# A GELU spelled out over three engines instead of one ScalarE activation, in a hybrid attention and state-space block

## The reference, cut to what matters

```python
y = s5_scan(u, ...)                    # includes the term d * u
z = jax.nn.gelu(y)                     # the tanh form
o_s5 = z * jax.nn.sigmoid(z @ w_glu[l] + b_glu[l])
branch_b = (o_s5 * jax.nn.silu(gate_s5)) @ w_proj_s5[l]
```

## Time and profile before

| | before |
|---|---|
| median of 3 runs | 458.5 us (458.2 to 458.8) |
| the profiled execution | 459.13 us, its span 457.3 us |
| TensorE busy | 422.7 us, 92% of the span |
| VectorE busy | 286.0 us, 63% |
| ScalarE busy | 201.8 us, 44% |
| GpSimd busy | 154.0 us, 34% |
| clock granted to TensorE, mean | 0.985 of full |

### The profile page before, as it was taken

The page is one execution under the profiler, slowest core; times in us unless marked ns, Lnnn a source line. Parts: engine busy times, 40 slices in busy tenths (PEclk is TensorE's granted clock), DMA queues, the critical chain, the costliest instruction groups (busy, mean ns, idle before and its releaser), DMA issues.

```text
span 457.3 us, 7138 instructions
## 1 busy us (share of the span) xinstructions
PE 422.7 (92%) x2715; PEld 338.5 (74%) x2715; DVE 286.0 (63%) x651; ACT 201.8 (44%) x392; POOL 154.0 (34%) x78
## 2 busy tenths in 40 slices
PE   0899999999999399889998999999999999999993
PEld 0888888889778376556665677888888888888993
DVE  1668679799989949988999784143062071080545
ACT  5651686922432147896545541222222222241433
POOL 0244442343242202242122324444544444444430
PEclk9999999999999599999999999999999999999998
DMA  8946996123941245100101103654333333323104
GB/s 252 247 105 158 136 252 178 42 72 92 273 89 54 47 71 163 46 1 1 47 1 47 47 2 92 219 175 113 92 92 93 92 93 94 111 95 115 47 3 182
DMA packets 72290, 47.27 MB, mean 103 GB/s; under 512 B 21208, under 2 KB 67744, under 8 KB 72224
## 3 DMA queue, kind: packets, MB, share of 16 engines
q1 hardware_dynamic: 71072, 46.74, 39.1%
q10 hardware_dynamic: 1184, 0.07, 0.2%
HBM read 42.61 MB, written 4.19 MB: 102 GB/s over the span
## 4 chain that ended last, share of the span: by engine, by line
PE 79%; DVE 8%; ACT 5%; issue 4%; DMA 2%; POOL 1%; POOLq 1%; SPq 0%; DVEq 0%; ACTq 0%
PE bank L919 22%; PE bank L921 21%; PE bank L920 21%; PE bank L1203 2%; PE bank L1224 2%; PE bank L1185 2%; DVE prob L1657 2%; PE bank L1083 2%; DMA x_sb<-in_x 2%; DVE prob L1677 1%; PE bank L967 1%; PE bank L1216 1%; ACT z L867 1%; ACT prob L861 1%; PE bank L1029 1%
## 5 line engine op out<-in xcount | busy, mean ns | idle before, releaser
L638 POOL TENSOR_TENSOR w_lo<-raw,w_hi 128x1024 fp32r<-128x1024 f32 (+2 forms) x56 | 134.6, 2404 | 239.6 <-ACT w_hi L668 239.6
L919 PE MATMUL bank<-hT_lo,w_hi 128*128 128x512 f32 x288 | 115.3, 400 | 0.9 <-ACT Y_sb L678 0.4
L921 PE MATMUL bank<-hT_hi,w_hi 128*128 128x512 f32 x288 | 112.4, 390 | 0.0
L920 PE MATMUL bank<-hT_hi,w_lo 128*128 128x512 f32 x288 | 112.3, 390 | 0.0
L668 ACT ACTIVATE w_hi<-raw 128x1024 fp32r<-128x1024 f32 (+2 forms) x56 | 58.4, 1043 | 74.8 <-PE bank L921 73.1
L919 PEld LDWEIGHTS bank<-hT_lo,w_hi 128*128 128x128 f32 x288 | 54.1, 188 | 14.4 <-issue 3.8
L921 PEld LDWEIGHTS bank<-hT_hi,w_hi 128*128 128x128 f32 x288 | 54.1, 188 | 11.7
L920 PEld LDWEIGHTS bank<-hT_hi,w_lo 128*128 128x128 f32 x288 | 54.1, 188 | 10.4
L861 ACT ACTIVATE prob<-prob,nmax 128x128 f32<-128x128 f32 (+2 forms) x64 | 35.3, 553 | 22.0 <-DVE nmax L1657 22.0
L883 ACT ACTIVATE tmp<-bank 128x512 f32<-128x512 f32 x16 | 9.5, 597 | 59.9 <-PE bank L921 57.5
L1719 DVE SCALAR_TENSOR_TENSOR tmp<-tmp,bank 128x512 f32<-128x512 f32 x8 | 5.5, 688 | 44.6 <-ACT tmp L883 44.6
(11 more groups left out here) (223 smaller groups left out, 735.7 us busy)
## 6 DMA issues: line engine op xcount, KB each, us to landing
raw<-in_w_in SPq DMA_DIRECT2D x28, 512.0 KB, 3.8
raw<-in_w_in SPq DMA_DIRECT2D x16, 256.0 KB, 3.7
raw<-in_w_out SPq DMA_DIRECT2D x8, 512.0 KB, 3.6
x_sb<-in_x SPq DMA_DIRECT2D x4, 512.0 KB, 5.8
raw<-in_w_proj_s SPq DMA_DIRECT2D x4, 512.0 KB, 3.5
raw<-in_w_proj_nsa SPq DMA_DIRECT2D x8, 256.0 KB, 3.8
r_sb<-in_x SPq DMA_DIRECT2D x1, 2048.0 KB, 9.6
out<-r_sb SPq DMA_DIRECT2D x8, 256.0 KB, 2.3
```

The source lines that it names most:

```text
L638: nc.gpsimd.tensor_tensor(lo, view(raw, block_at[name] % NRAW, wdims(name)), hi.bitcast(F32), ALU.subtract).then_inc(lo_done, 1)
L919: nc.tensor.matmul(dst, w[0], x[1], start=first, stop=False, skip_group_check=True)
L920: nc.tensor.matmul(dst, w[1], x[0], start=False, stop=False, skip_group_check=True)
L921: return nc.tensor.matmul(dst, w[0], x[0], start=False, stop=last, skip_group_check=True)
```

## The change

The one ScalarE activation with the GELU function is replaced by elementary steps, and its neighbours move:

- GpSimd takes three instructions for each tile: y squared, times a constant plus a constant, times y. They write the argument of the tanh into `z`, in chunk order. Each waits for the one ahead of it on a semaphore.
- ScalarE takes the tanh of `z` in place, with contiguous reads and writes, in steps 6 and 8 instead of 5 and 6.
- VectorE forms (1 + tanh) y in place in `yT`, in steps 7 and 9, and casts it to `z_hi` right behind, now reading contiguously and writing in token order.
- GpSimd then multiplies by the gate `sg_s5` into `z` and forms `z_lo`, one after the other for each tile. Both read one operand and write their result in token order.
- VectorE's multiplication by 2 and the gate in the GLU products goes away. The value in `z_hi` is twice the GELU, so the tanh of the GLU gets scale 0.25 instead of 0.5.

```diff
-D_TERM_AT, GELU_AT, Z_SPLIT_AT = (4, 5), (5, 6), (6, 7)
+D_TERM_AT, GELU_AT, Z_SPLIT_AT = (4, 5), (6, 8), (7, 9)
...
+            def gelu():
+
+                for t in range(4):
+                    pl.wait_ge(yd_done, t + 1)
+                    nc.gpsimd.tensor_tensor(z[:, t, :], yT[:, t, :], yT[:, t, :], ALU.mult).then_inc(y_squared, 1)
+                    pl.wait_ge(y_squared, 2 * t + 1)
+                    nc.gpsimd.tensor_scalar(z[:, t, :], z[:, t, :], GELU_SCALE * GELU_CUBE, GELU_SCALE, ALU.mult, ALU.add)\
+                        .then_inc(y_squared, 1)
+                    pl.wait_ge(y_squared, 2 * t + 2)
+                    nc.gpsimd.tensor_tensor(z[:, t, :], z[:, t, :], yT[:, t, :], ALU.mult).then_inc(gelu_arg, 1)
+                for t in range(4):
+                    wait_drained(pl, f"gs{t}")
+                    pl.wait_ge(zhi_done, t + 1)
+                    nc.gpsimd.tensor_tensor(tokens(z[:, t, :]), chunks(yT[:, t, :]), tokens(sg_s5[:, t, :]), ALU.mult)\
+                        .then_inc(z_gated, 1)
+                    nc.gpsimd.tensor_tensor(tokens(z_lo[:, t, :]), chunks(yT[:, t, :]), tokens(z_hi[:, t, :].bitcast(F32)),
+                                            ALU.subtract).then_inc(z_split, 1)
...
                 if name == "glu0":
-                    low_part(z_lo, z, z_hi, range(4), zhi_done, z_split)
+                    gelu()
...
-                nc.scalar.activation(tmp[:, 0, :], bk(job)[:, :], ACT.Tanh, scale=0.5, bias=bias).then_inc(th_done, 1)
+                nc.scalar.activation(tmp[:, 0, :], bk(job)[:, :], ACT.Tanh, scale=0.25 if kind == "glu" else 0.5, bias=bias)\
+                    .then_inc(th_done, 1)
...
-                        ac.wait_ge(yd_done, t + 1)
-                        nc.scalar.activation(z[:, t, :].rearrange("p (m j s) -> p s j m", s=CH, j=RUN),
-                                             yT[:, t, :].rearrange("p (s j m) -> p s j m", j=RUN, m=NRUN),
-                                             ACT.Gelu_apprx_tanh).then_inc(z_done, 1)
+                        ac.wait_ge(gelu_arg, t + 1)
+                        nc.scalar.activation(z[:, t, :], z[:, t, :], ACT.Tanh).then_inc(gelu_tanh, 1)
...
                 if kind == "glu":
 
+                    ve.wait_ge(z_gated, t + 1)
                     drain(V.scalar_tensor_tensor(out=z[:, t, :], in0=tmp[:, 0, :], scalar=1.0, in1=z[:, t, :],
                                                  op0=ADD, op1=MUL), job)
                     wait_drained(ve, job)
-
-                    wait_drained(ve, f"gs{t}")
-                    stt(z[:, t, :], z[:, t, :], 2.0, sg_s5[:, t, :], MUL, MUL)
...
+                        ve.wait_ge(gelu_tanh, t + 1)
+                        V.scalar_tensor_tensor(out=yT[:, t, :], in0=z[:, t, :], scalar=1.0, in1=yT[:, t, :],
+                                               op0=ADD, op1=MUL).then_inc(z_done, 1)
                         ve.wait_ge(z_done, t + 1)
-                        V.tensor_copy(z_hi[:, t, :], z[:, t, :]).then_inc(zhi_done, 1)
+                        V.tensor_copy(tokens(z_hi[:, t, :]), chunks(yT[:, t, :])).then_inc(zhi_done, 1)
```

More of the change, by code:

```diff
@@ L46 @@
 PI_C = TWO_PI - PI_A - PI_B
+GELU_CUBE = 0.044715
+GELU_SCALE = 0.7978845608028654
 COL = dict(q=0, kc=512, vc=640, ksl=768, vsl=896, kwi=1024, vwi=1152, gl=1280, gn=1304, u=1816, gs=2328,
@@ L383, in build_program, with tokens, chunks @@
         inv_done = sem("inverse_root_done")
+        y_squared, gelu_arg, gelu_tanh, z_gated = (sem(n) for n in ("y_squared", "gelu_argument", "gelu_tanh", "z_times_gate"))
         u_scr = nc.dram_tensor("u_scratch", (S5W, CH, NCH), F32, kind="Internal").ap()
         y_scr = nc.dram_tensor("y_scratch", (S5W, CH, NCH), F32, kind="Internal").ap()
+        def tokens(v):
+            return v.rearrange("p (m j s) -> p s j m", s=CH, j=RUN)
+        def chunks(v):
+            return v.rearrange("p (s j m) -> p s j m", j=RUN, m=NRUN)
         w4 = W[:, :, :, :].rearrange("p (q r) e c -> p r q e c", r=2)
```

## The result

The changed kernel takes 467.0 us (median of four runs, 465.7 to 467.4), the kernel before 458.65 (four runs, 458.2 to 459.3). The ratio is 1.0175 [1.0159, 1.0191]: slower by 8.4 us. The forecast was 473, slower by 14.5.

A forecast was written before the change was run, and what follows sets the result against it. VectorE, taking turns with GpSimd, was to bound the stretch before glu0: 22.4 + 2.8 + 1.0 + 16.3 + 1.1 = 43.6 us against 27.5, +16.1; GLU products -1.4; sum +14.7, 473 us (own range 466 to 479, whole range 460 to 484).

The forecast's parts named there:

- What bounds: From 188.6 to 216.1 us, TensorE, VectorE and ScalarE nearly full; with the change, VectorE's work and waits set the length.
- turn-taking: VectorE's SBUF-to-SBUF scalings and casts, and instructions with two SBUF inputs, alternate one for one with GpSimd's.
- The sum of the waits: VectorE's waits for GpSimd from 188.6 us to the start of glu0: 16.3 us, plus 1.1 for strided instructions.
- The rival with over 2 us: GpSimd's strided instructions take 2.4 us each, TensorE waits for z_split: +22, 481 us; chance 22%.
- the 1.95 of its ratio: Within the slow-strided rival: by the Trainium skill's ratio, 1.28 us would become 1.95, time near 476 us.
- the same formula: VectorE's length up to glu0: present work 22.4, new products 2.8, strided casts 1.0, waits 16.3 + 1.1: 43.6 us.
- The 3.8 of additional work on VectorE: Before glu0: four products with two SBUF inputs, 2.8 us, and casts that now write strided, 1.0 us.
- The GLU products: The product with the gate goes at four steps, 0.69 us each; on the chain in steps 14 and 17: -1.4.
- ScalarE's wait costs nothing: The tanh's wait for two tiles of arguments, at 197.6 us, is covered, since step 6's exponentials come later.
- One wait for a run: Rival, 17%: VectorE keeps its turn through a run; seven runs by about 0.8 us, +2.9: 461 us.
- GpSimd in the gaps: Rival, 7%: VectorE meets few GpSimd instructions, all waits together under 2 us; faster, 454 us.
- the third rival: TensorE's clock falls to 1.2 GHz after an idle stretch from 191.5 to 199: +3, 476 us; chance 6%.

The follow-up runs named there:

- that edit of two lines: The kernel before with the GELU of all four tiles in one step: 458.29 us (0.9996) in step 6, 456.73 us (0.9966) in step 8.
- the gate left out: The changed kernel without GpSimd's four multiplications by the gate: 464.15 us, ratio 1.0116 to the kernel before.
- both parts left out: The changed kernel without GpSimd's twelve argument instructions and its four gate multiplications: 459.27 us, ratio 1.0008 to the kernel before.
- the run with the GELUs in step 8: The kernel before with all four GELU tiles in step 8 and z_hi in steps 9 and 10: 456.73 us, ratio 0.9966.

## Why the prediction was right, and where its size was wrong

**What bounds, and turn-taking: right.** VectorE became the bound (28.95 of 29.23 us). The kernel before with twelve instructions on GpSimd whose results nobody reads shows the waits without the rest of the change.

**The sum of the waits: this step was mis-sized.** It was 16.3 and 1.1 for strided instructions, 17.4 us. The waits of the trace, each as its duration less the free one:

| run | forecast | measured |
|---|---|---|
| scalings of step 4, two D terms | 6.6 | 3.94 - 1.25 + 2.84 - 1.41 = 4.1 |
| scalings of step 5 | 1.9 | 2.38 - 0.87 = 1.5 |
| scalings of step 6 | 1.9 | 1.00 - 1.00 = 0 |
| first four of product and cast | 1.3 | 1.88 - 0.69 = 1.2 |
| scalings of step 7 | 1.9 | 3.60 - 1.25 = 2.35 |
| second four (second cast 1.82) | 1.3 | 1.82 - 0.63 = 1.2 |
| `oT_hi` and scalings of step 9 | 1.4 | 0.11 + 2.35 - 1.00 = 1.5 |
| sum | 16.3 + 1.1 | 11.8 |

The count of turns was right for all but one run. What was off is the length of a turn and, through it, when GpSimd is done. These are the groups of the changed kernel:

```profile
L655 POOL TENSOR_TENSOR z<-yT,sg_s 128x512 f32<-128x512 f32 x4 | 6.9, 1714 | 7.2 <-DVE z_hi L1734 7.2
L657 POOL TENSOR_TENSOR z_lo<-yT,z_hi 128x512 fp32r<-128x512 f32 x4 | 6.7, 1674 | 0.0
L651 POOL TENSOR_TENSOR z<-z,yT 128x512 f32<-128x512 f32 x4 | 5.4, 1350 | 0.3
L646 POOL TENSOR_TENSOR z<-yT 128x512 f32<-128x512 f32 x4 | 4.7, 1180 | 0.0
L648 POOL TENSOR_SCALAR z<-z 128x512 f32<-128x512 f32 x4 | 2.5, 621 | 0.3
```

The scalar form takes 0.62 us and not 0.9; I had taken the middle between MEMSET (0.53) and subtraction (1.28), and it lies close to the MEMSET. The square, which reads one tile twice, takes 1.04 when free and not 1.28. So a tile's three instructions are 2.9 us instead of 3.5, the twelve are over at 200.42 (199.14 + 1.28), and the scalings of step 6, which begin at 200.24, meet next to nothing of them. Step 4 lost 2.5 us of its forecast wait to the shorter turns, and step 6 all of its 1.9: 4.4 of the 5.6 us between 17.4 and 11.8. The strided form takes 1.52 to 1.83 us, where I had forecast 1.5. The rival with over 2 us is excluded, and the 1.95 of its ratio isn't reached either.

**The stretch: the same formula with the measured waits.** 22.4 + 3.8 + 11.8 = 38.0 us, where the trace has 37.7 (225.24 - 187.55). That it comes so close is partly luck. VectorE is busy only 36.62 of the 37.69 us, so it is idle for 1.1 us that the formula doesn't know. The work in the formula is in turn 1.4 us too long: 0.4 us of the 22.4 were a wait of the two scalings at 196.56 in the kernel before (1.43 us, 1.00 when free), and 1.0 us is not explained. The 3.8 of additional work on VectorE were right: products of 0.67 to 0.70 us, casts of 0.63 to 0.69. Against the kernel before it is +10.4 where +16.1 was forecast. That difference of 5.7 us is most of the error of the prediction (14.5 forecast, 8.4 measured). For the profiled execution 14.7 was forecast and 8.0 came, 6.7 less: the 5.7, and the 1.3 of its earlier start, which is no merit or fault of the forecast, less 0.3 of the GLU products.

**The GLU products.** Forecast -1.4, and from `z_lo` to the end the span is 1.1 us shorter. The three runs that leave a part of GpSimd's work out of the changed kernel have the same 1.0 to 1.1 us; no run isolates the product with the gate.

**ScalarE's wait costs nothing: right**, for the reason given. It stood 6.30 us for VectorE ahead of the exponentials of step 6, and the arguments were there when it had done them.

**The rivals.** One wait for a run is excluded: all four scalings of step 4 are long. GpSimd in the gaps is excluded, with waits of 11.8 us where 2 would decide. The clock did fall, as the third rival has it, twice: to the lower level (1.2 GHz, granted 0.50) behind the idle time of 4.84 us, and again behind that of 4.49 us. It doesn't go in place of the forecast but with it. The first cost nothing that can be seen, because VectorE was the bound with and without it. The second cost 1.1 to 1.5 us, since TensorE sets the pace there. A chance of 6% was too low for it, because I had seen the idle stretch coming and given it the same length as the one of the earlier trace rows.

**What would show it.** The four scalings were to take 1.2 to 1.6 us each: they took 0.82, 0.85, 1.37 and 1.15. GpSimd was to be busy 26 us with the twenty: 6.9 + 6.7 + 5.4 + 4.7 + 2.5 = 26.2, though for the wrong reason (shorter instructions, and their waits counted in). `z_lo` was to be first used near 232: 225.24. TensorE was to be idle some 20 us; between 187.55 and 225.24 it was 10.5 us, because the stretch is shorter and its matmuls at half clock count as busy.

## What to carry to other kernels

Before moving elementwise work to an idle GpSimd, list the VectorE instructions that run in the same microseconds, and mark those that scale or cast from SBUF to SBUF or have two SBUF inputs. Count one turn of GpSimd for each of them as long as GpSimd has work, and ask where that ends, because the length of GpSimd's instructions sets both the price and the number of turns. If what is to be saved is a table load, try first to gather the activations of the same table in one place, and in a step where nothing urgent is queued behind them on ScalarE: that edit of two lines gained 0.34% in one step and nothing in another, where the rewrite lost 1.75%.

## What the runs showed of the hardware

- The turn goes over to the other engine even when GpSimd's next instruction waits on a semaphore of its predecessor. Between the scalar form (ends 188.99) and the next (starts 189.07) there are 0.08 us, and VectorE still gets exactly one instruction a turn.
- Twelve GpSimd instructions that only write cost 0.38%, twelve that read cost 0.56% (the intervals overlap). The first kind lets instructions with two SBUF inputs run free and still delays scalings and casts.
- On GpSimd, 512 columns of float32 take 0.62 us in the scalar form, 1.04 for a product of a tile with itself, 1.27 with two inputs, and 1.52 to 1.83 with strided access.
- The length of TensorE's idle time alone didn't decide its clock. After 4.49 us (the changed kernel) and 3.22 us (the gate left out) the next matmuls ran at half clock. After 3.40 us (both parts left out) the next four ran at full clock and those behind them at half: 0.51 from 211.5 to 214.5. After 1.20 and 1.06 us, with 0.9 us of work between them, it was 0.57 in the run with the GELUs in step 8. After 1.19 and 1.05 us in the same place it stayed at 1.00 in the kernel before (244.0 to 248.0).
- The same matmuls, from the weighted values of step 10 to the first `z_lo`, took 6.24 us where the clock had stayed up, and 7.74 to 8.97 us where it had fallen.
